# Output projection, both norms and the first feed-forward tiles worked in parts of 256 tokens

## What is computed

```python
x = x + rms_norm(mixed @ w_out, norm_g[1])   # projection, norm, residual
hf = rms_norm(x, norm_g[2])                  # second norm
ff = jnp.square(jax.nn.relu(hf @ w_ff1)) @ w_ff2
```

## Time and profile before

| what | us |
|---|---|
| median of 3 runs | 3592.55 |
| span of the profiled execution | 3589.6 |
| PE busy | 3426.8 (95%) |
| DVE busy | 1920.1 (53%) |
| ACT busy | 1353.8 (38%) |
| POOL busy | 538.4 (15%) |
| last projection matmul to first feed-forward matmul, layer 0 | 23.7 |
| the same in the second block (768 tokens) | 37.7 |

### The profile page before, as it was taken

How to read it: one execution, slowest core, us unless ns; L and a number is a source line. 1 busy time by engine, 2 the same in 40 slices (tenths; PEclk the granted TensorE clock), 3 DMA queues, 4 the chain that set the end, 5 groups by cost and what they waited for, 6 DMA issues and landing times. The chain is left out here.

```text
span 3589.6 us, 46314 instructions
## 1 busy us (share of the span) xinstructions
PE 3426.8 (95%) x17878; PEld 2840.9 (79%) x17878; DVE 1920.1 (53%) x2315; ACT 1353.8 (38%) x1991; POOL 538.4 (15%) x376
## 2 busy tenths in 40 slices
PE   7999999999999999999998999999999999999998
PEld 5776878888777687888876888788888788868887
DVE  4374348777537333877755652533333656654445
ACT  3366234444336623444434443312212344333232
POOL 0031004333103100433311110100000100000000
PEclk9999999999999999999999999999999999999999
DMA  3201334443220123344310001121121021112222
GB/s 129 85 1 59 103 109 145 158 159 113 89 85 1 59 94 112 142 159 153 125 53 18 24 7 71 48 71 58 58 70 59 24 72 51 55 36 94 94 93 70
DMA packets 59475, 287.76 MB, mean 80 GB/s; under 512 B 10816, under 2 KB 12096, under 8 KB 32064
## 3 DMA queue, kind: packets, MB, share of 16 engines
q1 hardware_dynamic: 59328, 285.77, 22.8%
HBM read 283.64 MB, written 2.10 MB: 80 GB/s over the span
## 5 line engine op out<-in xcount | busy, mean ns | idle before, releaser
L162 PE MATMUL ps<-h_hi,w_hi_rest 128*128 128x512 f32 (+1 forms) x1072 | 385.2, 359 | 4.5 <-DVE h_lo L396 4.5
L163 PE MATMUL ps<-h_lo,w_hi_rest 128*128 128x512 f32 (+1 forms) x1072 | 363.4, 354 | 0.0
L1363 POOL TENSOR_TENSOR ada_context<-ada_context,ada_scaled 128x768 f32<-128x768 f32 x112 | 287.6, 2568 | 454.6 <-ACT ada_scaled L1447 449.4
L165 PE MATMUL ps<-h_hi,w_lo_rest 128*128 128x512 f32 (+1 forms) x1072 | 322.0, 355 | 0.0
L151 DVE TENSOR_TENSOR w_lo_mix<-w_raw,w_hi_mix 128x2048 fp32r<-128x2048 f32 x94 | 217.2, 2310 | 185.4 <-ACT w_hi_mix L145 185.3
L162 PE MATMUL ps<-h_hi,w_hi_mix 128*128 128x512 f32 x736 | 287.0, 390 | 4.5 <-DVE w_lo_mix L151 2.3
L435 POOL TENSOR_TENSOR x<-x,y 128x512 f32<-128x512 f32 (+1 forms) x32 | 64.5, 2017 | 1506.7 <-DVE y L441 1506.7
L163 PE MATMUL ps<-h_lo,w_hi_mix 128*128 128x512 f32 x736 | 286.5, 389 | 0.0
L165 PE MATMUL ps<-h_hi,w_lo_mix 128*128 128x512 f32 x736 | 286.5, 389 | 0.0
L1529 DVE TENSOR_TENSOR y<-ps,y 128x512 f32<-128x512 f32 (+1 forms) x224 | 165.9, 752 | 216.0 <-PE ps L165 215.2
L145 ACT ACTIVATE w_hi_rest<-w_raw 128x2048 fp32r<-128x2048 f32 x81 | 154.5, 1909 | 326.5 <-PE ps L165 315.5
(11 more groups left out here) (399 smaller groups left out, 7664.6 us busy)
## 6 DMA issues: line engine op xcount, KB each, us to landing
w_raw<-in_stream SPq DMA_DIRECT2D x205, 1024.0 KB, 4.9
ada_raw<-in_ada_w SPq DMA_DIRECT2D x128, 384.0 KB, 5.1
cmp_w<-in_cmp_w SPq DMA_DIRECT2D x8, 1024.0 KB, 4.9
mla_raw<-in_stream SPq DMA_DIRECT2D x8, 512.0 KB, 3.5
x<-in_x SPq DMA_DIRECT2D x1, 2048.0 KB, 8.7
out<-x SPq DMA_DIRECT2D x8, 256.0 KB, 2.0
x<-in_ctx SPq DMA_DIRECT2D x1, 1024.0 KB, 11.0
consts<-in_consts SPq DMA_DIRECT2D x1, 768.0 KB, 11.8
```

The source lines that it names most:

```text
L162: pe.matmul(out, whi, xhi, start=start, stop=False)
L163: pe.matmul(out, whi, xlo, start=False, stop=False)
L165: last = pe.matmul(out, wlo, xhi, start=False, stop=stop)
L1363: pool.tensor_tensor(ada.context, ada.context, ada.scaled[:, j % 2, :], ALU.add).then_inc(m["context"], 1)
```

## The change

`stage_project` is gone. A class `ProjectHead` works the projection and the start of the feed-forward in one block, and `Seam` holds the steps between them. The first 4 tiles of the projection run over all tokens as before. The other 4 run part by part, a part being 256 tokens: 2 parts in the first block, 3 in the second. The norm of one part is worked while PE multiplies the next: its four PE steps (sums and spread of either norm) stand at fixed places, ahead of steps 6, 10, 24 and 28 of the 32 steps (of three matmuls) of the next four tiles. The four first tiles of the feed-forward run part by part as well; the PE steps of the last part stand in those of part 0. The second norm's squares are added up by DVE in place of PE. The first unit of feed-forward weights is split into buffers of its own (`early`). `keep_busy` between the steps is gone. In the second block the clearing of semaphores now stands ahead of the projection, not behind it. SP loads the `ada` rows after the projection tiles (rows 0 to 3) and after the first two feed-forward tiles (rows 4 to 7), and the next unit of weights behind them.

```diff
+class Seam:
+    def pe_step(self, pe, p, step):
+        if step == 6:
+            self.pe_y_sums(pe, p)      # waits gathered; 2 matmuls acc x ones
+        elif step == 10:
+            self.pe_y_rows(pe, p)      # waits y_inverse; 2 matmuls
+        elif step == 24:
+            self.pe_x_sums(pe, p)      # waits x_gathered
+        elif step == 28:
+            self.pe_x_rows(pe, p)      # waits x_inverse
+    def dve_x_gather(self, dve, p, t):
+        if t == 0:
+            return
+        c = self.cols(p)
+        acc = self.k.acc[:, c]
+        dve.wait_ge(self.s["x_squared"], KT * p + t + 1)
+        ...
+        dve.tensor_tensor(acc, self.buffer(0, c) if t == 1 else acc, self.buffer(t, c), ALU.add).then_inc(self.s["x_gathered"], 1)
...
+class ProjectHead:
+    def pe(self, pe, ready):
+        ...
+        for p in range(self.n):
+            c = seam.cols(p)
+            for jj in range(4):
+                ...
+                for i in range(KT):
+                    if p:
+                        seam.pe_step(pe, p - 1, KT * jj + i)
+                    last = mm3(pe, [self.slot(p, jj)], *w[i], [(self.xhi[:, i, c], self.xlo[:, i, c])], i == 0, i == KT - 1)
+                last.then_inc(self.ready, 1)
+        for p in range(self.n):
+            for u in range(2):
+                ...
+                for i in range(KT):
+                    if p == 0:
+                        for odd in range(2):
+                            seam.pe_step(pe, self.n - 1, 2 * KT * u + 2 * i + odd)
+                    if u == 0:
+                        seam.pe_wait(pe, p, i)
+                    for m in range(2):
+                        ...
+                        last = mm3(pe, [k.ps[:, a:a + 256]], *w, [(k.hhi[:, i, c], k.hlo[:, i, c])], i == 0, i == KT - 1)
+                        if p == self.n - 1 and i == KT - 1:
+                            last.then_inc(ready, 1)
+    def dve(self, dve):
+        ...
+        for p in range(self.n):
+            more = p + 1 < self.n
+            for t in range(KT):
+                seam.dve_scale(dve, p, t)
+                if t % 2:
+                    seam.dve_add(dve, p, t - 1)
+                if more and t == 3:
+                    seam.dve_gather(dve, p + 1, 4)
+                if t >= 3:
+                    seam.dve_x_gather(dve, p, t - 3)
+            for t in range(KT - 3, KT):
+                seam.dve_x_gather(dve, p, t)
+            if more:
+                seam.dve_gather(dve, p + 1, 5)
+                seam.dve_gather(dve, p + 1, 6)
+            seam.dve_x_inverse(dve, p)
+            for t in range(KT):
+                seam.dve_h_scale(dve, p, t)
+                if t:
+                    seam.dve_h_lo(dve, p, t - 1)
+                if more and t == 3:
+                    seam.dve_gather(dve, p + 1, 7)
+                if more and t == 6:
+                    seam.dve_y_inverse(dve, p + 1)
+            seam.dve_h_lo(dve, p, KT - 1)
+            if p == self.n - 2:
+                split_lo(dve, k, n0 + 5)
...
@@ def stage_mlp(...), block.sync @@
+            if head is not None:
+                head.sync(sp)
             if ada:
+                sp.wait_ge(head.ready, head.tiles)
                 for j in range(KT):
+                    if j == KT // 2:
+                        sp.wait_ge(s["ready"], 2)
                     load_rows(0, j)
```

More of the change, by code:

```diff
@@ L1251, in stage_merge, with stage_mlp @@
     return n0 + UNITS_MERGE
[L1254 to L1304, removed]
+def stage_mlp(nc, k, name, stream, n0, y, hid_hi, hid_lo, tok, post, pre, last_unit, y_norm, head=None,
               ada=None):
@@ L1366, in _ @@
         def _(pe):
-            if post_norm is None:
+            if head is None:
                 n_post.pe_all(pe)
-            else:
[L1370 to L1373, removed]
+                n_pre.pe_all(pe, 9)
+                unit_ready(pe, k, n0)
+                first_tiles(pe, k, n0, 256, 2, tok, lambda i: normed.pe_wait(pe, i), s["ready"])
+            else:
+                head.pe(pe, s["ready"])
             def sum_rows(it, quarter):
@@ L1387, in group @@
             def group(it, first, last_group=False):
-                for j in range(2 if first else 0, T1 + T2):
+                for j in range((2 if head is None else T1) if first else 0, T1 + T2):
                     u = j // 2 if j < T1 else 2 + (j - T1) // 4
@@ L1434, in _ @@
         def _(act):
-            if post_norm is None:
+            if head is None:
                 n_post.act_all(act)
-            else:
-                n_post.act_root_columns(act)
-            n_pre.act_all(act, res.wait)
-            normed.act(act)
+                n_pre.act_all(act, res.wait)
+                normed.act(act)
+            else:
+                head.act(act)
+                act.wait_ge(s["ready"], 2)
             def scale_rows(it, j):
@@ L2646, in second_block @@
         rings(k, "rest", 175)
-        n = stage_project(nc, k, "mla_o", stream, n, k.hhi, k.hlo, y, TOK, UNITS_2, mla_norm, pause=14)
     with k.sem_scope():
-        n = stage_mlp(nc, k, "mlp0", stream, n, y, hid_hi, hid_lo, TOK, parts_of(b, 0, 1, TOK), parts_of(b, 0, 2, TOK, 3), UNITS_2,
-                      mlp_norm, mla_norm)
+        per_part = [(b.sc[:, 1, :, v], b.sc[:, 2, :, v], b.mod[:, 3, :, v]) for v in (0, 0, 1)]
+        mla_o = ProjectHead(k, "mla_o", stream, n, k.hhi, k.hlo, y, TOK, UNITS_2, per_part,
+                            (at("mlp_first_hi", [P, UNIT], F32R, 114), at("mlp_first_lo", [P, UNIT], F32R, 122)), pause=14)
+        n = stage_mlp(nc, k, "mlp0", stream, n + 4, y, hid_hi, hid_lo, TOK, None, None, UNITS_2, mlp_norm, mla_o)
         stage_residual(nc, k, "mlp0r", y, TOK, parts_of(b, 0, 3, TOK), mlp_norm, gate_norm, units=((n, 1024), (n + 1, UNIT)))
@@ L2803, in first_block @@
         n = stage_merge(nc, k, b, stream, n)
-        wo_norm, ff_norm = Norm(k, "wo_norm", y, KT, SEQ, 4), Norm(k, "ff_norm", y, KT, SEQ, 4)
-        n = stage_project(nc, k, "wo", stream, n, b.mhi, b.mlo, y, SEQ, UNITS_1, wo_norm, 1)
-        n = stage_mlp(nc, k, "ff", stream, n, y, hid_hi, hid_lo, SEQ,
-                      [(0, SEQ, b.g[:, 1, :])], [(0, SEQ, b.g[:, 2, :], None)], UNITS_1, ff_norm, wo_norm, ada)
+        ff_norm = Norm(k, "ff_norm", y, KT, SEQ, 4)
+        wo = ProjectHead(k, "wo", stream, n, b.mhi, b.mlo, y, SEQ, UNITS_1, [(b.g[:, 1, :], b.g[:, 2, :], None)] * 2,
+                         (b.ff_hi, b.ff_lo), 1)
+        n = stage_mlp(nc, k, "ff", stream, n + 4, y, hid_hi, hid_lo, SEQ, None, None, UNITS_1, ff_norm, wo, ada)
         assert n == UNITS_1
```

260 lines of the change are left out of this document (249 added, 11 removed).

## The result

The changed kernel takes 3631.96 us (median of 4 runs, 3631.38 to 3633.28) beside 3592.05 for the kernel before on the same chip (3590.39 to 3594.09). The ratio is 1.0117, with a 95% interval of 1.0102 to 1.0131. That is 40 us slower, where 3609 us (3581 to 3625) was predicted. The profiled execution has a span of 3629.6 us.

The account below looks back on a forecast made before the run. PE, busy 95%, was taken as the bound, with only 85.1 us of gaps to win. Two layer seams costing 18.8 us, less 2.6 won in the second block, add 16.2 to 3592.55: 3609 us, range 3581 to 3625.

Parts of the forecast that it names:

- On DVE the way from that split's start to the last `hid_lo` was 10.04 us, POOL's collisions in it; so 20.1.: Behind layer 0's seam: DVE's old 10.04 us chain is kept, ending 20.1 us after the first two feed-forward tiles.
- The wait for the unit: At the second matrix's first unit in layer 0: PE idle about 8 us, released by DVE's split.
- I charge 2 us for it: Behind the 5.2 us wait at part 1's sums: clock drops to 1.2 GHz, costing 2 us (bounds 0 and 2.9).
- I take 1.0 a part: In each part's scaling phase on DVE: collisions with POOL's adds cost 1.0 us (bounds none and 2.2).
- Rival 3: DVE and POOL exclude each other at every add (8 us), four more clock drops of 2 us: 3625; chance 0.12.
- The seam of layer 0: From projection to feed-forward: seam gives back 2.3 us, but late work behind it makes it cost 9.4, two 18.8.
- The second block: Its three-part seam: 8.1 us less, 1.6 back for the next unit, 3.9 for the boundary; 2.6 us won.
- The boundary: Before the second block's projection: the 4.17 us boundary leaves the old gap, giving 3.9 us back.
- 1: Seam waits happen without collisions (7 us) or clock loss (8 us): 3594, no change; chance 0.18.
- 2: No collisions or clock loss, unit no hindrance (4.9 x 2), cheaper SBUF adds (6 us), or a shorter chain: 3578; chance 0.20.

Follow-up runs that it names:

- Experiment 9: Changed kernel with POOL's seven ada adds of group 0 cut to 8 of 768 columns (part of the sums left out): 3616.48 us.
- Experiment 4: Changed kernel with 26 idle matmuls ahead of each of the second norm's seven sums, place unchanged: 3623.66 us.
- experiments 1: Changed kernel with the first two weight units of the second matrix issued ahead of ada rows 4 to 7 in the first block: 3616.61 us.
- 3 to 7: Changed kernel with sums at step 31, 3621.74 us; idle matmuls, 3623.66; units first, ada work later, late sums, 3613.21; these plus idle matmuls, 3609.65; only second block changed, 3593.63.
- 10: Kernel of experiment 6 with POOL's seven ada adds of group 0 cut to 8 of 768 columns (part of the sums left out): 3577.35 us.
- experiment 8: Changed kernel with all eight adds to x in the seams on DVE, none on POOL: 3627.62 us.
- Experiment 11: Kernel before with only the second block changed, its second-norm sums at step 31 and 10 idle matmuls ahead of each: 3582.96 us.
- experiment 6: Changed kernel with units loaded first, ada work behind hidden slices, sums at step 31 and 10 idle matmuls ahead of each: 3609.65 us.

## Why the prediction was wrong, step by step

The direction was right, and the waits were forecast at their places with their releasers. The sum was 23 us short: 18.6 in the two layers (37.4 where 18.8 was forecast) and 4.6 in the second block. Three terms of it were mis-sized.

**"On DVE the way from that split's start to the last `hid_lo` was 10.04 us, POOL's collisions in it; so 20.1."** This is the step that failed. I carried over a duration that held two collisions (the latent of 2.60 us, and 2.32 us in the earlier trace rows; some 1.6 us too long each) to a place where POOL's adds fall beside all six operations. It took 16.2 us. Measured: the split starts 11.1 us after the two tiles (565.69 - 554.6; 10.0 was predicted), and the last `hid_lo` ends at 27.3. Experiment 9 shows that 9.4 of the 16.2 us are POOL's, where the 10.04 had held 3.2. What the sum had not asked is what POOL would be fed by: before, ACT waited for the fourth tile and so gave POOL a pause just when DVE needed SBUF; now the four tiles come before the unit, and there is no pause. Besides, PE had 10.9 us of tiles left behind the first two before, and has 5.8 us now; and the rows 4 to 7 must wait for those two tiles, since their buffers share memory with those of `early`, with the unit's load behind them. The wait for the unit came near the forecast (7.74 us, where about 8 was said), but that was luck: the terms of the sum give 10.0 + 2.3 - 5.8 = 6.5.

**"I charge 2 us for it"**, once in a seam of the layers and once or twice in the second block. The clock fell behind all seven waits of `L529` (4.22 to 5.50 us; PEclk 0.56 to 0.70 over the 5.6 us behind each), in the first parts too, and again behind the late unit (0.54), as it had before at 4.17 us. In layer 0 the two tiles were ready 50.45 us after the end of part 0's projection (504.15 to 554.6), where 47.7 was predicted; that part's projection had ended 1.6 us late, since its first matmuls ran at half rate (0.43 us each, 469.27 to 471.98), which I had not foreseen. That is no part of the change: in experiments 1, 3 to 7 and 10 the same matmuls ran at full rate. Experiment 4 shows that the drops at the sums cost more than 6 us over the kernel.

**"I take 1.0 a part"** for collisions in the scaling phase. It was 3 x 0.53 = 1.6. Rival 3 had the mechanism in full, with four collisions; three came. Of its other part, more drops of the clock, those behind the sums of the first parts came; behind the wait of 2.6 us for the unit, which measured 2.10, there was none (PEclk 1.00). The Trainium skill (SBUF — State Buffer, Who interferes with whom) states that a DVE operation with two SBUF inputs and a GpSimd operation that reads SBUF exclude each other for the whole instruction. The sum that waited until POOL was done, the latent of 2.0 us beside the copy of 0.68, and experiment 8 all agree with it.

**The seam of layer 0.** The sum of the three: the second tile of the second matrix ended at S + 115.2 (469.27 to 584.5) against 104.0, and before at 94.6. That is 20.6 of the 21.3 us of the milestone. Of the 11.2 us by which the forecast missed here, 1.6 lie ahead of the seam, 2.75 in it, and 6.9 behind the two tiles (29.9 us, where 23.0 was predicted). Layer 1 lost only 16.1; its waits were 4.22, 0.15, 2.09 and 5.48 us in the seam and 8.63, 4.01 and 1.66 behind it. Some 1.4 us of the difference are the slow matmuls at S, which layer 1 does not have; why the rest differs was not tried.

**The second block.** 2.6 us to be won, 2.0 lost. The boundary came as predicted: PE was idle 5.84 us ahead of the projection, in place of 2.16, which is 3.7 us more where 3.9 was forecast. The waits at the sums were 4.60, 4.75 and 5.49 us with a drop each. Experiment 11 moves the block to the other side of zero by removing nearly all of these.

**Rivals.** 1 and 2 needed waits without drops of the clock and a unit that is in time; neither was so. 2's idea, that a chain which is less late would win, holds in the second block only.

## What to carry to other kernels

When a seam is made shorter, ask what starts at a fixed event behind it, and lay its work out beside that of the engine with which it takes turns: a duration read from the old trace holds only the collisions of the old order. Count POOL's adds and the DVE operations that have all their inputs in SBUF as one queue. And a step in the order of a busy engine belongs where its input is ready, or behind idle work of just the length of its wait: in this kernel a wait of 4.2 to 5.5 us cost itself, and then about half of the next 4 to 5 us.

## What the runs showed of the hardware

- DVE and POOL took turns at SBUF, and operations with a PSUM input were free of it: a latent of 768 columns took 2.0 to 2.6 us beside POOL's adds and 1.0 alone, a sum of 256 columns 0.95 and 0.42; a copy from PSUM took 0.68 both ways.
- POOL's own adds were drawn out in the same way: 7 of 768 columns took 16.99 us beside DVE, 2.4 each, where the shortest of the 112 in the kernel after took 1.91.
- The granted clock stayed at 1.00 behind a wait of 2.10 us and fell to 0.50 behind waits of 3.33, 4.22, 4.60, 5.50 and 7.8 us. In the seam of the kernel after it was back at 1.00 within 5.6 us; behind the 7.8 us at the ada sums of experiment 6 it was not for 15 us (582.75 to 597.70, PEclk 0.51).
- A single long wait was not needed for it. In experiment 6 PE was idle for 1.10 us and, 3.4 us later, for 1.48 us. Behind the second, PEclk was 0.50 from 540.38 to 545.00, and the matmuls started 0.21 us apart in place of 0.12:

```profile
537.02 0.61 PE L529 MATMUL ps<-consts,acc 128*128 128x1 f32 x4 [1.10 <-DVE acc L541]
540.38 0.58 PE L162 MATMUL ps<-h_hi,ff_first_hi 128*128 128x256 f32 x1 [1.48 <-DVE h_lo L630]
```
